# A hybrid layer on one core: three places reordered on VectorE, a store put ahead of loads, and projection pieces issued in halves

## The reference, cut to what matters

```
proj = x @ w_in
y_sb   = stick_breaking_attention(q, k, v) * silu(g_sb)      # 4 heads of 128, causal, blocks of 128 keys
y_pool = multiscale_pool(u, w_pool, scale) * silu(g_pool)    # 4 groups, window 2, 4, 8, 16
y_lru  = rg_lru(u, conv, gates) * silu(g_lru)                # 4 groups of 128; a linear recurrence over the rows
y_xa   = memory_cross_attention(q, mem) * silu(g_xa)         # 4 heads
merged = sum over n of sigmoid(merge_n) * (y_n @ w_branch[n])
out = layer_norm(alpha * x + merged @ w_out)
# in rg_lru:  h[t] = a[t] * h[t-1] + mult[t] * (i[t] * xc[t])
```

## Time and profile before

| | |
|---|---|
| median of 3 runs | 2468.97 us (2468.85 to 2471.33) |
| the profiled execution's own time | 2470.5 us |
| its span from the first to the last instruction | 2468.7 us |
| PE busy | 2396.3 us, 97% of the span |
| DVE, ACT, POOL busy | 1583.4, 1170.4, 1225.7 us |
| mean granted clock of TensorE | 0.993 |

### The profile page before, as it was taken

How to read it: one execution, slowest core, us unless ns; L and a number is a source line. 1 busy time by engine, 2 the same in 40 slices (tenths; PEclk the granted TensorE clock), 3 DMA queues, 4 the chain that set the end, 5 groups by cost and what they waited for, 6 DMA issues and landing times.

```text
span 2468.7 us, 30065 instructions
## 1 busy us (share of the span) xinstructions
PE 2396.3 (97%) x10480; PEld 1921.4 (78%) x10480; DVE 1583.4 (64%) x1996; ACT 1170.4 (47%) x1835; POOL 1225.7 (50%) x759
## 2 busy tenths in 40 slices
PE   8999999999999999999899999999999989999998
PEld 5877778878877888888677777678878867888887
DVE  6677752864596476468777777832764596476466
ACT  4566642343474245233477677742342474245220
POOL 1566643764465344443555555543764465344431
PEclk9999999999999999999999999999999999999999
DMA  4543222123213322372433333222124213322352
GB/s 192 175 124 124 91 103 90 52 77 128 92 45 115 124 61 86 105 279 78 129 97 105 100 114 103 65 93 90 52 77 133 88 45 115 125 60 86 103 196 77
DMA packets 130550, 258.67 MB, mean 105 GB/s; under 512 B 13024, under 2 KB 75488, under 8 KB 129376
## 3 DMA queue, kind: packets, MB, share of 16 engines
q1 hardware_dynamic: 128960, 252.02, 30.9%
q10 hardware_dynamic: 1440, 4.72, 0.6%
HBM read 197.97 MB, written 58.72 MB: 104 GB/s over the span
## 4 chain that ended last, share of the span: by engine, by line
PE 86%; DVE 6%; issue 4%; ACT 2%; POOL 1%; DMA 1%; SPq 0%; POOLq 0%; DVEq 0%; ACTq 0%
PE J L701 17%; PE J L703 17%; PE J L702 17%; PE Z L868 7%; PE OB L838 4%; PE ACC L868 4%; PE OB L868 4%; PE Z L701 2%; PE Z L702 2%; PE Z L703 2%; PE ACC L816 1%; PE ACC L818 1%; PE ACC L826 1%; PE ACC L828 1%; DVE PS L1858 1%
## 5 line engine op out<-in xcount | busy, mean ns | idle before, releaser
L701 PE MATMUL J<-XBH,WHS 128*128 128x512 f32 x1152 | 454.4, 394 | 13.5 <-issue 10.7
L702 PE MATMUL J<-XBL,WHS 128*128 128x512 f32 x1152 | 450.5, 391 | 0.0
L703 PE MATMUL J<-XBH,WLS 128*128 128x512 f32 x1152 | 450.4, 391 | 0.0
L2119 POOL TENSOR_TENSOR WLS<-SR,WHS 128x1024 fp32r<-128x1024 f32 x132 | 358.0, 2712 | 176.9 <-ACT WHS L1023 168.7
L701 PE MATMUL J<-XBH,WH 128*128 128x512 f32 x864 | 343.3, 397 | 16.5 <-DVE XBL L1556 5.1
L703 PE MATMUL J<-XBH,WL 128*128 128x512 f32 x864 | 337.5, 391 | 0.0
L702 PE MATMUL J<-XBL,WH 128*128 128x512 f32 x864 | 337.3, 390 | 0.0
L701 PEld LDWEIGHTS J<-XBH,WHS 128*128 128x128 f32 x1152 | 217.2, 189 | 68.0 <-issue 16.5
L2156 POOL TENSOR_TENSOR PLO<-PF,PHI 128x512 fp32r<-128x512 f32 (+3 forms) x160 | 198.6, 1242 | 136.2 <-DVE PHI L1744 132.8
L703 PEld LDWEIGHTS J<-XBH,WLS 128*128 128x128 f32 x1152 | 217.3, 189 | 46.3
L702 PEld LDWEIGHTS J<-XBL,WHS 128*128 128x128 f32 x1152 | 217.5, 189 | 44.1
(11 more groups left out here) (358 smaller groups left out, 5172.6 us busy)
## 6 DMA issues: line engine op xcount, KB each, us to landing
RAW<-w SPq DMA_DIRECT2D x144, 512.0 KB, 3.7
pk_m<-MB SPq DMA_DIRECT2D x56, 512.0 KB, 5.2
MB<-pk_m SPq DMA_DIRECT2D x48, 512.0 KB, 4.1
KR<-pk_k SPq DMA_DIRECT2D x160, 128.0 KB, 2.2
BRAW<-w SPq DMA_DIRECT2D x64, 256.0 KB, 4.7
VR<-pk_v SPq DMA_DIRECT2D x160, 64.0 KB, 2.0
XRAW<-xt SPq DMA_DIRECT2D x8, 1024.0 KB, 13.0
OR<-w SPq DMA_DIRECT2D x16, 512.0 KB, 7.7
```

The costliest lines, as they stand in the source:

```text
L701: nc.tensor.matmul(to, wh, xh, start=first, stop=True, skip_group_check=True)
L702: nc.tensor.matmul(to, wh, xl, start=False, stop=True, skip_group_check=True)
L703: return nc.tensor.matmul(to, wl, xh, start=False, stop=True, skip_group_check=True)
L2119: G_.tensor_tensor(WLS[:, k, :], SR[:, k, :], WHS[:, k, :].bitcast(F32), ALU.subtract).then_inc(s_lo, 1)
```

## The change

Six edits, none of which changes what is computed.

1. **The third merge.** The recurrence's input gate `(LI + 1) * XC` gets a function of its own, `input_gate`, that runs after `variance` of the same group, a pair before `recur`; `recur` has one product less. The first `YL` of merge 2 is made at the end of the pair before; `rest_of_first` of pair `M2 + 2` is put behind the last `YL`.
2. **The last pooled group.** Level 3 of `windows` runs after piece 13's sum, not before it.
3. **The second half's first head.** SP's `last_rows` goes from piece 6 to piece 2 of the second pair, `first_keys` from 10 to 13 (in the first half too, where only `first_keys` does something). In that pair `rest_of_first` runs on DVE after piece 9's sum instead of after piece 6.
4. **Pieces in halves.** PE issues the filling of the attention heads by inner block (`halves_filled`); the other engines keep whole pieces.
5. **The last head of the second half.** Its filling has six halves more in the first three steps, and fewer later.
6. **The last rows.** The border between DVE and ACT with POOL goes from column 512 to 768.

```diff
+LAST = 768
...
+def halves_filled(half, h, s):
+
+    n = 2 * PIECES * (2 if h + 1 < HEADS else 1)
+    if half and h + 1 == HEADS:
+        lead = 2 * LEAD + 2 * min(s + 1, SUMS)
+        return min(n, lead + (n - 2 * (LEAD + SUMS)) * max(s + 1 - SUMS, 0) // NS[half])
+    return min(n, 2 * LEAD + (n - 2 * LEAD) * (s + 1) // (NS[half] + SUMS))
 def filled(half, h, s):
-    n = PIECES * (2 if h + 1 < HEADS else 1)
-    return min(n, LEAD + (n - LEAD) * (s + 1) // (NS[half] + SUMS))
+    return halves_filled(half, h, s) // 2
...
-                pair(g0 + 1, {6: last_rows, 10: first_keys})
+                pair(g0 + 1, {2: last_rows, 13: first_keys})
...
-                    for g, i in fill[filled(half, h, s - 1):filled(half, h, s)]:
-                        piece(g, i)
+                    for k in range(halves_filled(half, h, s - 1), halves_filled(half, h, s)):
+                        piece(*fill[k // 2], (k % 2,))
...
-                if i == 6 and l + 1 < PAIRS and not quiet(g + 1):
+                if i == (9 if l == 1 else 6) and l + 1 < PAIRS and l != M2 + 1 and not quiet(g + 1):
                     rest_of_first(g + 1)
...
-                    hooks = {1: lambda: recur(half, HEADS - 1), 5: lambda: rest_y(half, n, (0, 1)),
-                             9: lambda: rest_y(half, n, (2, 3))}
+                    hooks = {1: lambda: recur(half, HEADS - 1), 5: lambda: rest_y(half, n, (1,)),
+                             9: lambda: (rest_y(half, n, (2, 3)), rest_of_first(g0 + 2))}
...
+            def input_gate(half, h):
+                hh = half * HEADS + h
+                dve.wait_ge(l_sig, 4 * hh + 4)
+                dve.wait_ge(xc_f, hh + 1)
+                link(V_.scalar_tensor_tensor(LI[h][:], LI[h][:], 1.0, XC[h % 2][:], ALU.add, ALU.mult))
             def recur(half, h):
...
-                link(V_.scalar_tensor_tensor(r, LI[h][:], 1.0, r, ALU.add, ALU.mult))
-                link(V_.scalar_tensor_tensor(r, r, 0.5 * ROOT_DOWN, XC[h % 2][:], ALU.mult, ALU.mult))
+                link(V_.scalar_tensor_tensor(r, r, 0.5 * ROOT_DOWN, LI[h][:], ALU.mult, ALU.mult))
...
-                n = C if r == HALVES * TB - 1 else D
+                n = LAST if r == HALVES * TB - 1 else D
...
-                    hooks = {9: lambda: windows(half, h, (0, 1)), 11: lambda: windows(half, h, (2, 3)),
-                             13: lambda: differences(half, h)}
+                    hooks = {9: lambda: windows(half, h, (0, 1)), 11: lambda: windows(half, h, (2,)),
+                             13: lambda: (windows(half, h, (3,)), differences(half, h))}
...
-                                             convolved(half, h))
+                                             convolved(half, h), input_gate(half, h - 1))
...
-                                             variance(half, HEADS - 1)),
-                                })
+                                             variance(half, HEADS - 1), input_gate(half, HEADS - 1),
+                                             rest_y(half, 2, (0,)))})
```

More of the change, by code:

```diff
@@ L703, in pass3, with block_product @@
                 return nc.tensor.matmul(to, wl, xh, start=False, stop=True, skip_group_check=True)
-            def block_product(to, w, w0, b, first):
-                for k in range(2):
+            def block_product(to, w, w0, b, first, ks):
+                for k in ks:
                     mm = pass3(to[:], (w[0][:, w0 + k, :], w[1][:, w0 + k, :]), (XBH[b][:, k, :], XBL[b][:, k, :]),
@@ L712, in _, with piece @@
             ONE, SUMMED, TWO = (WH1, WL1), (WHS, WLS), (WH2, WL2)
-            def piece(g, i):
+            def piece(g, i, ks=(0, 1)):
                 a, c, d = J[g % 2], J[(g + 1) % 2], J[2]
@@ L721, in piece @@
                     pe.wait_ge(x_lo, NU * half + LO_ORDER[half].index(i) + 1)
-                if i == 0:
+                if ks[0]:
+                    pass
+                elif i == 0:
                     pe.wait_ge(a_lo, g + 1)
@@ L748, in piece @@
                              (d, TWO, 0))[i // 2]
-                mm = block_product(to, w, w0 + i % 2 * 2, i, i in (0, 2, 4, 12))
+                mm = block_product(to, w, w0 + i % 2 * 2, i, i in (0, 2, 4, 12), ks)
+                if ks[-1] == 0:
+                    return
                 if i % 2:
@@ L1503, in scale_last @@
                     t = TB - 1
-                    upper = RES[t % 3][:, C:D]
+                    upper = RES[t % 3][:, LAST:D]
                     nc.scalar.mul(upper, upper, LN[t % 2][:, L_INV:L_INV + 1]).then_inc(scaled, 1)
@@ L1900, in recur @@
                 dve.wait_ge(l_root, hh + 1)
-                dve.wait_ge(l_sig, 4 * hh + 4)
-                dve.wait_ge(xc_f, hh + 1)
                 r = LR[h][:]
-                link(V_.scalar_tensor_tensor(r, LI[h][:], 1.0, r, ALU.add, ALU.mult))
-                link(V_.scalar_tensor_tensor(r, r, 0.5 * ROOT_DOWN, XC[h % 2][:], ALU.mult, ALU.mult))
+                link(V_.scalar_tensor_tensor(r, r, 0.5 * ROOT_DOWN, LI[h][:], ALU.mult, ALU.mult))
                 link(V_.tensor_copy(SM2[:, 0:1], HSTATE[:, h:h + 1]))
@@ L2231, in finish_last @@
                 pool.wait_ge(scaled, 1)
-                r = RES[(TB - 1) % 3][:, C:D]
-                G_.tensor_tensor(r, r, LNB[:, C:D], ALU.add).then_inc(o_rest, 1)
+                r = RES[(TB - 1) % 3][:, LAST:D]
+                G_.tensor_tensor(r, r, LNB[:, LAST:D], ALU.add).then_inc(o_rest, 1)
             for half in range(HALVES):
```

## The result

The changed kernel takes 2454.99 us (median of 4 runs, 2454.46 to 2456.13) against 2470.15 (4 runs of before on the same chip, 2468.85 to 2473.26): ratio 0.9936, 95% interval 0.9925 to 0.9948. It is faster, as forecast, but by 15 us and not by 31, and 2455 lies outside the range 2427 to 2453. The profiled execution took 2456.13 us, its span is 2454.3, 14.4 less than before.

The account below looks back on a forecast made before the run. PE bounds the kernel, busy 2396.3 of 2468.7 us; gains come from its idle time and low clock. Terms 12.1 + 1.4 + 6.1 + 6.7 + 4.6 + 0.4 = 31.3 gave a median of 2438 us, range 2427 to 2453.

Parts of the forecast that it names:

- The third merge and the other recurrences, 12.1 + 1.4: Third merges: PE starts 3.5 us earlier per half, plus clock, 12.1; other recurrences: DVE-to-PE loop 0.35 shorter four times, 1.4.
- the clock's 5.1: Third merges of both halves: low clock behind the `YL` waits gone, 2.4 + 2.7 us, assuming none behind the remaining 1.6.
- The last pooled group, 6.1: Last pooled group: PE's waits of 2.2 us gone in both halves, 4.4, plus 1.7 of low clock in the first.
- The second half's first head, 6.7: Second half's first head: 4.2 for `PLO`, 1.0 at the transposes, 2.3 of clock, less 0.5 and 0.3 for key loads.
- Pieces in halves and the last head, 4.6: Attention heads: 2.1 us of `PLO` waits at the last head's start covered, plus 2.5 of other small waits.
- The rival on the halves: Heads: PE reaches pieces' first halves too early, about 65 pieces wait; at 0.7 us each 2484, slower; chance 0.03.
- three pieces in the first three steps cover the 2.1: Second half's last head: 18 matmuls, over 4 us, cover the 2.1 us wait for `PLO` at its start.
- The 2.5 taken from the small waits: Heads' steps without filling: half of 5.1 us of other waits goes, since half as many steps stay bare.
- The end, 0.4: Last rows: POOL's 256 columns take 0.63 us from 2464.5 and end at 2465.1 instead of 2465.6.
- only the stores and the pooled group pay: Rival: the reordered merge brings nothing and new low-clock stretches take more; 2450 to 2463 us; chance 0.07.
- The port moves the loss: Rival at the third merge: DVE falls behind POOL's port use, `YL` wait over 2 us remains; 2447; chance 0.2.
- The signs named in advance: Forecast is wrong if `YL` takes over 4 us, low stretches appear in new places, or `KR` or `J` waits in heads.

Follow-up runs that it names:

- the load moved: Second half's first head's part alone on the kernel before, with the 512 KB weight tile's load issued behind the first keys: 2464.69 us (-6.3).
- halves where they pay: Kernel before with pieces in halves in the second half's heads alone, spread evenly to the end: 2465.74 us (-5.3).
- the four corrections: Changed kernel with whole pieces in first half's heads, even last-head spread, first keys' loads ahead of weight tile, input gate at recurrence's start: 2441.75 us, ratio to before 0.9885.
- the best: Changed kernel with whole pieces in first half's heads, even last-head filling, keys' loads ahead of weight tile, gate at recurrence's start: 2441.75 us; with gate early 2443.04.
- the late gate: Input gate again at the start of `recur`, regrouping kept: 2453.15 us on the changed kernel; 2458.03 with the third merge's part alone on the kernel before.

## Why the prediction was wrong in size, and what of it held

The forecast of 31.3 us was 21.8 of PE's waits, 9.1 of the clock and 0.4 at the end. The traces show 10.6, 3.3 and 0.5. The parts alone gain 8.3, 1.5, 6.7 and -1.0, 15.5 in all; together 15.2. Each is known to some 3 us, so this close a match is partly luck, but no large loss lies between the parts: the error is in single terms of the sum.

- **The third merge and the other recurrences, 12.1 + 1.4: measured 8.3.** The mechanism of the merge was right. Its waits (for `ST` and `YL`) fell from 6.3 to 3.2 in the first half and from 5.9 to 3.4 in the second with this part alone, 3.1 and 2.5 where 3.5 each was forecast. The new wait for `ST` was forecast as 0.7 and is 0.79 and 1.58 in the changed kernel, 1.33 and 1.60 in the part alone. The recurrence's one product takes 1.21 and starts later; the last two `YL` are blocked by POOL's operations again:

```profile
750.96 1.23 DVE L1815 TENSOR_TENSOR YL<-Y,YH 128x1024 fp32r<-128x1024 f32 x1
752.10 0.68 DVE L1605 TENSOR_TENSOR ST<-J,ST 128x512 f32<-128x512 f32 x1
752.70 2.78 DVE L1629 TENSOR_TENSOR WL<-RAW,WH 128x512 fp32r<-128x512 f32 x1
755.41 1.21 DVE L1923 SCALAR_TENSOR_TENSOR LR<-LR,LI 128x1024 f32<-128x1024 f32 x1
...
765.02 3.43 DVE L1815 TENSOR_TENSOR YL<-Y,YH 128x1024 fp32r<-128x1024 f32 x2
```

  The wait left for `YL` was forecast as 1.6 and is 1.86 and 1.70. The step that failed is the clock's 5.1, by "I assume no low clock behind so short a one". Behind the first half's 1.86 the clock is low, for half as long as before; behind the second half's it is not. And what came back was not kept: with this part alone two new low stretches stand at 1528 and 1801 us, behind waits of 2.15 that the trace of before has too, without one, and cost 1.65 each. PE's busy time fell by only 0.3 (2396.3 to 2396.0). The part's trace is 8.2 shorter, by 7.9 of idle time, above all 5.6 at the merges, the 1.2 for `LU` told of above, and 1.6 at the second half's first head, whose wait for `PLO` is 2.6 there and not 4.2, for a reason that no run separates. That the new low stretches are the edit's doing is not shown. The 1.4 for the other recurrences is not there: the early gate turns two waits in the pairs into one of about the same sum.
- **The last pooled group, 6.1: measured 5.9 in the stages, 6.7 alone.** Right.
- **The second half's first head, 6.7: measured 1.5.** The old waits went (4.16 and 1.93, and the low clock behind them). The step that failed is "I take 0.5 us of waiting here and 0.3 in the first half (0 to 1 each)": the waits for keys are 2.25 and 2.15. I counted the loads' queueing behind two transfers, too low in the first half, and not that SP itself stops at the first of them until a buffer is free. With the load moved the part gives 6.3.
- **Pieces in halves and the last head, 4.6: measured -1.0.** Two steps failed. The rival on the halves named PE reaching a first half too early, but spread that loss thinly over 65 pieces and got a chance of 0.03, on the ground that PE never waits in the heads' middle. A busy PE shows only that no wait is due at the old places, not how much slack the next one has. It was one piece in each of three heads, 1.5 each. And "three pieces in the first three steps cover the 2.1" held for the wait named, but 1.21 came back at the next `ARG`, while the thinner rest uncovered a clash that cost 2.30 and a low stretch behind it. The 2.5 taken from the small waits for `ARG` was right: they fell from 4.3 to 1.8. With halves where they pay the part gives 5.3.
- **The end, 0.4: measured 0.5.** Right in size, not in its working. From PE's last product to the span's end it is 8.12 and not 8.59, in every kernel with this edit. POOL's 256 columns take 1.01 and not the 0.63 of proportion, but they start sooner: they lie from 2450.18 to 2451.19 beside DVE's 768 columns, which end at 2450.61. That fits the blocking of the two engines seen elsewhere; POOL's `PLO` of 256 columns takes 0.73.

With the four corrections the parts alone give 12.7 + 6.3 + 6.7 + 5.3 = 31.0 and together 29.1 by the medians (30.0 in the trace: 22.6 of idle time, 6.9 of busy time, 0.5 at the end). So a gain of the size forecast could be had, with four other placements; that does not make the forecast right for this change. The signs named in advance (waits for `KR` and `J` in the heads, low stretches in new places) are those that came. Of the rivals, "only the stores and the pooled group pay" has 2455 in its range and the new low stretches, but its mechanism did not come: the merge brought most of all, the reordered stores 1.5. "The port moves the loss" was near in kind, but the merge, of which it spoke, behaved; "the halves wait too early" had the mechanism at three pieces and not at 65. ACT's wait for `pk_v` is 1.92, where I named 1.5 as the bound.

What stays open is the price of the early gate: 4.5 by the medians on the kernel before, 1.8 on the changed one, 1.3 and unresolved on the best. Added up over the last recurrent pairs and the third merges of both halves, PE's waits are 17.1 on average in the eight traces with the part and the early gate (15.3 to 18.4), and 15.8 in the three with the late one (14.2 to 17.6). By the medians the late gate is never the worse, so no gain of the early one is shown, and the regrouping, the early `YL` and the deferred `WL` carry the part; which of these three does how much was not tested.

## What to carry to other kernels

Before a DMA is moved behind another on the same queue, ask what the one ahead waits for: the queue stops there, whatever the bytes. Splitting filler work brings its first part forward; look, for each part, at the wait that guards it and at what stands behind it in that engine's program, since an engine at 100% says nothing of the slack. And the terms whose mechanism was followed in the trace came out close (the pooled group, the waits at the merge), while those that assumed that nothing new would wait (the keys, the halves, the clock) did not: these deserve the widest bounds.

## What the runs showed of the hardware

A conversion on DVE with a single SBUF input is blocked by POOL as two-input products are: `PHI<-PF` of 128x256 takes 2.34 beside POOL's `WLS`, and 0.56 for 128x512 elsewhere. The page SBUF — State Buffer of the Trainium skill, section "Who interferes with whom", names DVE's faster copy modes beside operations with two inputs as those that need the shared port, and the trace fits that.

The granted clock is at its lower level for 30.7 us of the trace of before up to PE's last product, 20.5 of the changed kernel's and 13.7 of the best, but 37.5 with the second half's halves alone, a kernel that is faster than before all the same. In all 17 traces each such stretch begins within a PE wait of at least 1.8 us or at most 1.7 us behind it (89 stretches); but there are 170 such waits (17 of them at the program's start), so little more than half have one. The same wait of 2.15 at the second half's last pooled group is followed by one in five traces (+1.6 us for the stage) and by none in two, that of before among them. Such a stretch costs only the part in which PE has work: of the 30.7 us before PE was busy for 25.2, of the 20.5 after for 18.8, and half the difference is 3.2, close to the 3.3 that its busy time fell by. My four clock terms summed to 9.1. A term for the clock is a chance for each wait, which ends only with the wait itself.
